# The end of the router in another order, and products of ones behind the last expert

## The chip, the cores and the metric

The kernel runs on one core of a Trainium2 chip, as one program. TensorE (PE) does matrix products and turns tiles (a transpose is a product with the identity), VectorE (DVE) and ScalarE (ACT) work elementwise, GpSimd (POOL) and SyncE (SP) mostly start DMAs. The metric is the device time of one execution in microseconds, the median of several.

## What is computed

A decoder trunk of two layers over 576 tokens (512 of a prompt, 64 of samples), 1024 wide. The part that the change touches is the hierarchical mixture of experts, which follows the mixer in each layer:

```
x = layer_norm(ALPHA * x + mix)                     # x1
g_logits = x @ w_group + b_group                    # 4 groups
e_logits = x @ w_expert + b_expert                  # 16 experts
g_idx = argmax(g_logits)
top_vals, top_idx = top_k(e_logits of group g_idx, 2)
hgu = x @ w_gate_up[e];  a = silu(gate) * up * combine;  y = sum over e of a @ w_down[e]
x = layer_norm(ALPHA * x + y)                       # x2
x = x + sigmoid(x @ w_gate + b) * (p[i] @ w_proj)   # gate products, projection
```

## The kernel before

Every product is made in float32 quality from two halves of each operand (`hi`, the rounded part, and `lo`, the rest), as three products: ACT makes `w_hi` or `x_hi`, DVE subtracts to get `lo`. The program is written by hand for each engine: each engine has its own list of instructions, works through it strictly in the written order, and waits on semaphores (`wait_ge`). So the order of the calls below is the order in time.

The mixer's last products are made token by token (`out_rows`). The 576 tokens are five tiles, 0 to 3 of 128 tokens and 4 of 64. For tile i TensorE does `row_turns(i)` (x added by a turn), then `row_products(i, h, ...)` for the two halves h of the 1024 columns, 12 products each. Then follows the router for that tile:

- DVE: `stats_of(i)` and `norm_of(i)`, the layer norm, which gives `x_tok` (semaphore `normed`, `nz_ok`); ACT supplies the square root in between (`std_tile`).
- PE: `h_turns(i)` turns the 128 x 1024 rows into PSUM banks 4 and 5, which all tiles share, so it waits until the tile before is out of them (`hl_ok`).
- ACT: `rows_hi(i)` copies out `x1T_hi`; DVE: `rows_lo(i)` subtracts to `x1T_lo`.
- PE: `logits(i)`, 16 narrow products. Tiles 0 and 1 are group 0, tiles 2 to 4 group 1 (`GROUPS`).
- for a group g: ACT `logits_copy(g)`, PE `logit_turns(g)`, DVE the choice of experts (`select`: comparisons, places, one-hot marks), PE `ranks(g)` (a running count of the tokens of each expert), DVE `slots_of(g)`, PE `slot_products(g)`. They end in `slot_token` (`idx`), the list of which token stands in which slot of which expert.

With that list POOL gathers the 128 rows of the first expert from `x_scratch` into `x_gathered` (an indirect DMA), PE turns them (`turn_slots`), and the 16 experts begin (`gate_up`). While the router has TensorE wait, the projection of `p` (eight tiles of 12 products, `proj_half`/`proj`, copied out by ACT in `proj_out`) fills in: tiles 1 and 0 before and around the last logits, tile 2 around the slot products, tiles 3 to 6 while the gather is under way, tile 7 behind `turn_slots`.

The weights of the experts come in units of 1 MB. SP starts a load when DVE has split the unit that stood in the slot (`split_done`), so the loads follow the pace of the other engines.

Behind the last expert, `last_rows` adds the last two experts' rows on TensorE, DVE and ACT make the second layer norm tile by tile (`add_rows`, `row_mean`, `squares`, `std_of`, `rstd2`), TensorE turns the tiles (`n2_turn_rows(i)`), DVE and ACT scale them into `xT` and split them, and the sixteen `gate(q)` products of 24 matmuls each follow. `n2_turn_rows(2)` stands behind `gate(1)`, `n2_turn_rows(3)` behind `gate(4)`.

Of the kernel before, what the change touches and what calls it, by code (L numbers as in the profile page):

```python
# [79 lines left out]
def trunk(nc, x_in, outs):  # L80
# [228 lines left out]
    with ctx:  # L309
# [38 lines left out]
        ht_ok, hh_ok, hl_ok = sem("x1_turned"), sem("x1T_hi_ready"), sem("x1T_lo_ready")  # L348
        lt_cp, lt_ok = sem("logits_copied"), sem("logits_turned_back")
# [64 lines left out]
        def rows_bank(i):  # L414
            return 2 * (i % 2)
# [11 lines left out]

        def p_parts(dst, g):
# [70 lines left out]

        TR_IN = 0  # L500
# [346 lines left out]
        def _(act):  # L847
# [74 lines left out]
            for l in range(DEPTH):  # L922
# [10 lines left out]

                def proj_out(mo):
                    act.wait_ge(mt_done, M_P[l] + (1, 0, 2, 3, 4, 5, 6, 7).index(mo) + 1)
                    act.activation(halves(ppT[:, mo, :]), pair(mo % 2), ACT.Copy).then_inc(pp_done, 1)
# [31 lines left out]
                rows_hi(4)  # L968
                logits_copy(1)
                proj_out(1)  # L970
                proj_out(0)
                hi(U_E[l] + 1)
                proj_out(2)
                hi(U_E[l] + 2)
                for mo in range(3, KT - 1):
                    proj_out(mo)
# [186 lines left out]
        def _(dve):  # L1163
# [149 lines left out]
            for l in range(DEPTH):  # L1313
# [23 lines left out]

                def p_low(g):
# [7 lines left out]

                lg20 = lg[:, :, :, :].rearrange("p t g j -> p t (g j)")

                def select(a, b):
# [12 lines left out]
                    for c, (op, mask) in enumerate(((ALU.is_ge, earlier), (ALU.is_gt, later))):  # L1362
# [4 lines left out]
                                              in_=won.rearrange("p q c i -> p q (c i)"), op=ALU.add, axis=AX.X))  # L1367
                    place = rank_c[:, 5 * a:5 * b, :].rearrange("p (t g) j -> p t g j", g=5)
# [358 lines left out]
        def _(pe):  # L1727
# [170 lines left out]
            def out_rows(l, gl_n, pair_sem, pair_n, d):  # L1898
# [48 lines left out]

                def logit_turns(g):
# [384 lines left out]
```

## Time and profile before

| | |
|---|---|
| median of 3 runs | 1281.59 us (1281.4 to 1281.94) |
| the profiled execution: time, span | 1281.04 us, 1279.5 us |
| PE busy | 1227.1 us, 96% of the span |
| DVE busy | 834.9 us, 65% |
| ACT busy | 558.0 us, 44% |
| chain that ended last, by engine | PE 71%, DVE 13%, DMA 10%, ACT 3% |
| mean granted clock of TensorE | 0.983 |

A row of the timeline gives the start in us from the span's start, the length in us, the engine, the line of the kernel and the operation, and in brackets the time the engine was idle before it and what ended that.

### The profile page before, as it was taken

The page shows a single profiled execution, that of the slowest core. Times are in us where ns is not written, and L with a number is a line of the kernel's source. Part 1 is how long each engine was busy: PE and PEld are TensorE (multiplying, and loading weights), DVE is VectorE, ACT ScalarE, POOL GpSimd, SP SyncE. Part 2 cuts the span into 40 slices and gives each one's busy share as a digit, 9 for nine tenths or more (in the row PEclk, how much of TensorE's full clock was granted, in tenths as well). Part 3 has the DMA queues.
Part 4 walks back from the last instruction along what each step waited for, and adds up shares of the span by engine and source line. Part 5 has one row for each costly group of instructions (what it writes and reads, how often), then busy time and mean ns, then how long its engine had stood idle before and what let it go on. Part 6 is the DMA issues. An engine that isn't in the chain of part 4 may idle for free.

```text
span 1279.5 us, 19633 instructions
## 1 busy us (share of the span) xinstructions
PE 1227.1 (96%) x7659; PEld 1115.6 (87%) x7659; DVE 834.9 (65%) x1118; ACT 558.0 (44%) x627; POOL 164.0 (13%) x193
## 2 busy tenths in 40 slices
PE   7999999999999999899999799999999899999798
PEld 6888899999999998788878599999998788877598
DVE  4554477464474737789889785445434778989783
ACT  4322232213131222378787564112121368878651
POOL 2200010010000002013231001000002012232100
PEclk9999999999999999799999899999999899999899
DMA  9444254243242322469998553322312359999512
GB/s 337 153 158 156 104 158 144 93 150 119 78 152 73 126 77 101 161 259 378 374 377 302 195 168 101 99 67 93 105 69 85 141 198 366 388 396 346 211 50 75
DMA packets 85616, 229.76 MB, mean 180 GB/s; under 512 B 9798, under 2 KB 42702, under 8 KB 73136
## 3 DMA queue, kind: packets, MB, share of 16 engines
q1 hardware_dynamic: 66880, 179.84, 38.9%
q0 software_dynamic: 18672, 49.04, 10.8%
q8 instruction: 44, 0.72, 0.2%
q14 instruction: 20, 0.16, 0.0%
HBM read 210.15 MB, written 35.46 MB: 192 GB/s over the span
## 4 chain that ended last, share of the span: by engine, by line
PE 71%; DVE 13%; DMA 10%; ACT 3%; issue 2%; POOL 1%; DVEq 0%; SPq 0%; POOLq 0%; ACTq 0%
PE ps L1739 14%; PE ps L1741 14%; PE ps L1740 14%; DMA w_raw<-in_moe_w_gate_up 7%; PE ps L1790 3%; PE ps L1792 3%; PE ps L1791 3%; DVE w_lo L1169 3%; PE ps L2077 2%; PE ps L2079 2%; PE ps L2078 2%; ACT w_hi L853 2%; PE ps L1850 2%; DVE x_tok L1568 2%; PE ps L2041 1%
## 5 line engine op out<-in xcount | busy, mean ns | idle before, releaser
L1169 DVE TENSOR_TENSOR w_lo<-w_raw,w_hi 128x2048 fp32r<-128x2048 f32 (+1 forms) x133 | 290.5, 2191 | 70.4 <-ACT w_hi L853 69.6
L1739 PE MATMUL ps<-x_hi,w_hi 128*128 128x288 f32 (+2 forms) x1024 | 306.4, 299 | 8.8 <-DVE x_lo L1613 7.1
L1741 PE MATMUL ps<-x_hi,w_lo 128*128 128x288 f32 (+2 forms) x1024 | 303.9, 297 | 0.0
L1740 PE MATMUL ps<-x_lo,w_hi 128*128 128x288 f32 (+2 forms) x1024 | 303.9, 297 | 0.0
L853 ACT ACTIVATE w_hi<-w_raw 128x2048 fp32r<-128x2048 f32 (+1 forms) x133 | 242.7, 1834 | 79.3 <-PE ps L1741 61.6
L1739 PEld LDWEIGHTS ps<-x_hi,w_hi 128*128 128x128 f32 x1024 | 195.0, 190 | 9.9 <-issue 7.5
L1740 PEld LDWEIGHTS ps<-x_lo,w_hi 128*128 128x128 f32 x1024 | 194.9, 190 | 0.1
L1741 PEld LDWEIGHTS ps<-x_hi,w_lo 128*128 128x128 f32 x1024 | 194.8, 190 | 0.0
L1739 PE MATMUL ps<-g_hi,w_hi 128*128 128x288 f32 x384 | 114.8, 299 | 3.4 <-DVE g_full L1715 2.7
L1741 PE MATMUL ps<-g_hi,w_lo 128*128 128x288 f32 x384 | 113.9, 296 | 0.0
L1740 PE MATMUL ps<-g_lo,w_hi 128*128 128x288 f32 x384 | 113.7, 296 | 0.0
L2077 PE MATMUL ps<-w_hi,xgT_hi 128*128 128x512 f32 x256 | 103.1, 403 | 6.7 <-DVE xgT_lo L1460 6.5
L2079 PE MATMUL ps<-w_hi,xgT_lo 128*128 128x512 f32 x256 | 100.2, 391 | 0.0
L2078 PE MATMUL ps<-w_lo,xgT_hi 128*128 128x512 f32 x256 | 99.7, 390 | 0.0
L1790 PE MATMUL ps<-w_hi,x_hi 128*128 128x512 f32 x192 | 75.8, 395 | 3.5 <-DVE w_lo L1180 3.5
L1739 PEld LDWEIGHTS ps<-g_hi,w_hi 128*128 128x128 f32 x384 | 72.7, 189 | 5.0 <-DVE g_full L1715 2.9
L1169 DVE TENSOR_TENSOR w_lo<-w_raw_more,w_hi 128x2048 fp32r<-128x2048 f32 x30 | 68.1, 2291 | 13.0 <-ACT w_hi L853 13.0
L1792 PE MATMUL ps<-w_hi,x_lo 128*128 128x512 f32 x192 | 75.4, 393 | 0.0
L1791 PE MATMUL ps<-w_lo,x_hi 128*128 128x512 f32 x192 | 75.3, 392 | 0.0
L1254 DVE TENSOR_TENSOR gate_sum<-ps,b_spatial 128x512 f32<-128x512 f32 x24 | 16.5, 690 | 89.2 <-PE ps L1852 89.2
L1741 PEld LDWEIGHTS ps<-g_hi,w_lo 128*128 128x128 f32 x384 | 72.7, 189 | 0.0
L1740 PEld LDWEIGHTS ps<-g_lo,w_hi 128*128 128x128 f32 x384 | 72.7, 189 | 0.0
(295 smaller groups left out, 2123.3 us busy)
## 6 DMA issues: line engine op xcount, KB each, us to landing
w_raw<-in_moe_w_gate_up SPq DMA_DIRECT2D x34, 1024.0 KB, 11.0
w_raw<-in_moe_w_down SPq DMA_DIRECT2D x32, 1024.0 KB, 13.8
w_raw_more<-in_moe_w_gate_up SPq DMA_DIRECT2D x30, 1024.0 KB, 14.3
w_raw<-in_a_w_in SPq DMA_DIRECT2D x23, 1024.0 KB, 5.2
w_raw<-in_a_w_out SPq DMA_DIRECT2D x12, 1024.0 KB, 5.1
w_raw<-in_b_w_in SPq DMA_DIRECT2D x12, 1024.0 KB, 5.2
w_raw<-in_ple_w_gate SPq DMA_DIRECT2D x8, 1024.0 KB, 11.9
v_scratch<-v_stage POOLq DMA_DIRECT2D x6, 1024.0 KB, 4.5
```

The lines of the kernel that those rows point to most:

```text
L853: act.activation(unit_of(whi, d), raw_unit(d), ACT.Copy).then_inc(hi_done, 1)
L1169: dve.tensor_tensor(unit_of(wlo, d), raw_unit(d), unit_of(whi, d).bitcast(f32), ALU.subtract).then_inc(split_done, 1)
L1568: ch.link(dve.scalar_tensor_tensor(out=xtok[0:t, i, :], in0=yrows(i, t, k), scalar=wtop[0:t, k, i:i + 1], in1=xtok[0:t, i, :], op0=ALU.mul ...
L1739: pe.matmul(out, sh, mh, start=first, stop=False)
L1740: pe.matmul(out, sh, ml, start=False, stop=False)
L1741: ins = pe.matmul(out, sl, mh, start=False, stop=final)
L1790: pe.matmul(v_bank(i), xh_, wh, start=first, stop=False)
L1791: pe.matmul(v_bank(i), xh_, wl, start=False, stop=False)
L1792: ins = pe.matmul(v_bank(i), xl_, wh, start=False, stop=final)
L2077: pe.matmul(ps[:, 0, :], xs[0], ws[0], start=(a == 0 and k == 0), stop=False)
L2078: pe.matmul(ps[:, 0, :], xs[0], ws[1], start=False, stop=False)
L2079: ins = pe.matmul(ps[:, 0, :], xs[1], ws[0], start=False, stop=(a == 1 and k == 3))
```

## The change

At the router's end the order is rewritten on three engines, in both layers. On PE `h_turns(3)` goes between the two halves of the row products of tile 4, `logit_turns(0)` just ahead of it. On DVE `rows_lo(3)` goes ahead of the norm of tile 4. `select` is cut in two, `places_of` and `marks_of`, and the marks of group 0 come behind the norm of tile 4. The tile 4 is normed, turned, copied, subtracted and multiplied in two halves of 512 columns, with a semaphore for each first half (`norm_last`, `last_turns`, `last_rows_hi`, `last_rows_lo`, `last_logits`). The projection's tiles run in the order 1, 0, 3, 2, 4 to 7; tile 3 comes ahead of the ranks, so that tiles 4 to 6, not 3 to 6, stand between the slot products and `turn_slots`. Behind the last expert 6, 6 and 12 products of ones with ones, 512 columns wide, are written into PSUM bank 0; nothing reads them, and the first of `gate(0)` overwrites the bank.

```
+        PROJ_ORDER = (1, 0, 3, 2, 4, 5, 6, 7)
...
+                def last_rows_hi():
+                    act.wait_ge(r_mm, NT * l + NT - 2)
+                    for h, (turned_ok, done) in enumerate(((ht_half, hh_half), (ht_ok, hh_ok))):
+                        act.wait_ge(turned_ok, (l + 1) if h == 0 else NT * (l + 1))
+                        act.activation(hTh[0][:, 4 * h:4 * h + 4, 0:TS], turned_half(h), ACT.Copy).then_inc(done, 1)
...
+                def norm_last():
...
+                    for h, done in enumerate((nz_half, nz_ok)):
+                        c = slice(512 * h, 512 * h + 512)
+                        dve.scalar_tensor_tensor(out=xtok[0:TS, i, c], in0=xtok[0:TS, i, c], scalar=rstd[0:TS, i:i + 1], in1=lnp[0:TS, 1, c],
+                                                 op0=ALU.mult, op1=ALU.add).then_inc(done, 1)
...
-                select(*GROUPS[0])
+                places_of(*GROUPS[0])
+                rows_lo(3)
                 stats_of(4)
-                norm_of(4)
-                rows_lo(3)
-                rows_lo(4)
+                norm_last()
+                marks_of(*GROUPS[0])
+                last_rows_lo()
                 slots_of(*GROUPS[0])
-                select(*GROUPS[1])
+                places_of(*GROUPS[1])
+                marks_of(*GROUPS[1])
                 slots_of(*GROUPS[1])
                 lo(U_E[l] + 1)
...
                 h_turns(2)
+                row_products(4, 0, range(ROUND))
                 logit_turns(0)
-                row_products(4, 0, range(ROUND))
+                h_turns(3)
                 row_products(4, 1, range(ROUND)).then_inc(mt_done, KT - NT + 1)
-                h_turns(3)
                 pe.wait_ge(pl_ok, 3 * l + 3)
                 logits(2)
-                ranks(0)
-                pe.wait_ge(nz_ok, 2 * NT * l + NT - 1)
                 proj_half(l, 1, 0)
                 proj_half(l, 1, 1).then_inc(mt_done, 1)
-                h_turns(4)
                 logits(3)
-                logits(4)
-                pe.wait_ge(nz_ok, 2 * NT * l + NT)
+                last_turns()
+                ranks(0)
                 proj_half(l, 0, 0)
+                last_logits()
+                proj_half(l, 0, 1).then_inc(mt_done, 1)
                 logit_turns(1)
-                proj_half(l, 0, 1).then_inc(mt_done, 1)
+                pe.wait_ge(pp_done, KT * l + 1)
+                proj_half(l, 3, 0)
+                proj_half(l, 3, 1).then_inc(mt_done, 1)
+                pe.wait_ge(pp_done, KT * l + 2)
+                proj_half(l, 2, 0)
                 ranks(1)
                 slot_products(0)
-                pe.wait_ge(pp_done, KT * l + 2)
-                proj_half(l, 2, 0)
+                proj_half(l, 2, 1).then_inc(mt_done, 1)
                 slot_products(1).then_inc(ab_used, 1)
-                proj_half(l, 2, 1).then_inc(mt_done, 1)
-                for mo in range(3, KT - 1):
+                for mo in range(4, KT - 1):
                     proj(l, mo)
                 turn_slots(l, 0, bank=4)
                 proj(l, KT - 1)
...
+                def keep_running(n):
+                    for _ in range(n):
+                        pe.matmul(ps[:, 0, :].rearrange("p (a t) -> p a t", t=P), ones_r[:, :],
+                                  ones_r[:, :].unsqueeze(1).to_broadcast([P, 4, P]), start=True, stop=True)
+
+                pe.wait_ge(atl_ok, NE * (l + 1))
+                keep_running(6)
                 n2_turn_rows(0)
+                keep_running(6)
                 n2_turn_rows(1)
-                pe.wait_ge(atl_ok, NE * (l + 1))
+                keep_running(12)
                 for q in range(GQ):
                     gate(q)
```

On DVE, at the router's end, the order was as follows, from the marks of group 0 to the ranks of its slots (`x1T_lo_121` and `x1T_lo_120` are the lower halves of the turned rows of tile 3 and of tile 4):

```order
L1372 SCALAR_TENSOR_TENSOR expert_onehot<-places,group_onehot 128x32
L1375 SCALAR_TENSOR_TENSOR choice_onehot<-places,group_onehot 128x32 x2
L1379 TENSOR_TENSOR choice_rows<-choice_onehot,row_value 128x32 x2
L1322 BN_STATS v_stats<-ps 64x6 x2
L1324 BN_AGGR mean_var<-v_stats 64x2
L1330 SCALAR_TENSOR_TENSOR x_tok<-ps,mean_var,ln_params 64x1024
L1333 RECIPROCAL rstd<-rstd 64x1
L1335 SCALAR_TENSOR_TENSOR x_tok<-x_tok,rstd,ln_params 64x1024
L1345 TENSOR_TENSOR x1T_lo_121<-ps,x1T_hi_119 128x1024
L1345 TENSOR_TENSOR x1T_lo_120<-ps,x1T_hi_118 128x8x64
L1389 TENSOR_TENSOR choice_values<-choice_onehot,ps 128x32 x2
```

and it is now:

```order
L1371 TENSOR_TENSOR x1T_lo_121<-ps,x1T_hi_119 128x1024
L1335 BN_STATS v_stats<-ps 64x6 x2
L1337 BN_AGGR mean_var<-v_stats 64x2
L1354 SCALAR_TENSOR_TENSOR x_tok<-ps,mean_var,ln_params 64x1024
L1357 RECIPROCAL rstd<-rstd 64x1
L1361 SCALAR_TENSOR_TENSOR x_tok<-x_tok,rstd,ln_params 64x512 x2
L1404 SCALAR_TENSOR_TENSOR group_onehot<-places,valid 128x8
L1407 SCALAR_TENSOR_TENSOR expert_onehot<-places,group_onehot 128x32
L1410 SCALAR_TENSOR_TENSOR choice_onehot<-places,group_onehot 128x32 x2
L1414 TENSOR_TENSOR choice_rows<-choice_onehot,row_value 128x32 x2
L1376 TENSOR_TENSOR x1T_lo_120<-ps,x1T_hi_118 128x4x64 x2
L1424 TENSOR_TENSOR choice_values<-choice_onehot,ps 128x32 x2
```

The tile 3 is subtracted ahead of the statistics of tile 4 and no longer behind its norm, the marks of group 0 stand behind the norm in place of ahead of it, and the last scaling and the last subtraction are two instructions each.

On PE, between the row products of tile 4 (`w_hi,g_hi`), the turns (`x_tok`) and the logits, the list was:

```order
L1935 MATMUL ps<-ident,x_tok 128x128 x8
L1953 MATMUL ps<-ident,logits_turned 128x64 x2
L1915 MATMUL ps<-w_hi,g_hi 64x512
L1916 MATMUL ps<-w_lo,g_hi 64x512
...
L1916 MATMUL ps<-w_lo,g_hi 64x512
L1917 MATMUL ps<-w_hi,g_lo 64x512
L1935 MATMUL ps<-ident,x_tok 128x128 x8
L1944 MATMUL ps<-x1T_hi_118,w_router_hi_lo 64x128
```

and it is now:

```order
L1972 MATMUL ps<-ident,x_tok 128x128 x8
L1952 MATMUL ps<-w_hi,g_hi 64x512
L1953 MATMUL ps<-w_lo,g_hi 64x512
...
L1954 MATMUL ps<-w_hi,g_lo 64x512
L2007 MATMUL ps<-ident,logits_turned 128x64 x2
L1972 MATMUL ps<-ident,x_tok 128x128 x8
L1952 MATMUL ps<-w_hi,g_hi 64x512
L1953 MATMUL ps<-w_lo,g_hi 64x512
```

The turn of tile 3 stands ahead of the second twelve products in place of behind them, and the turn of the logits of group 0 behind the first twelve in place of ahead of them.

On PE, behind the last expert (`last_onehot` are the marks of `last_rows`, `x_tok` the rows that `n2_turn_rows` turns, `x_hi` and `w_hi` the first gate products), the list was:

```order
L2135 MATMUL ps<-expert_y,last_onehot 128x512 x8
L2197 MATMUL ps<-ident,x_tok 128x128 x16
L1739 MATMUL ps<-x_hi,w_hi 128x256
L1740 MATMUL ps<-x_lo,w_hi 128x256
L1741 MATMUL ps<-x_hi,w_lo 128x256
```

and it is now, with the products of ones:

```order
L2189 MATMUL ps<-expert_y,last_onehot 128x512 x8
L2286 MATMUL ps<-ones_r 128x512 x6
L2251 MATMUL ps<-ident,x_tok 128x128 x8
L2286 MATMUL ps<-ones_r 128x512 x6
L2251 MATMUL ps<-ident,x_tok 128x128 x8
L2286 MATMUL ps<-ones_r 128x512 x12
L1776 MATMUL ps<-x_hi,w_hi 128x256
L1777 MATMUL ps<-x_lo,w_hi 128x256
L1778 MATMUL ps<-x_hi,w_lo 128x256
```

One run of 16 transposes is now cut into two of 8, with unread products ahead of each and behind.

## Rows read from the trace of the kernel before

**Rows 1.** The page, part 4: the chain's share of the span by line.
```profile
...
PE ps L1739 14%; PE ps L1741 14%; PE ps L1740 14%; DMA w_raw<-in_moe_w_gate_up 7%; PE ps L1790 3%; PE ps L1792 3%; PE ps L1791 3%; DVE w_lo L1169 3%; PE ps L2077 2%; PE ps L2079 2%; PE ps L2078 2%; ACT w_hi L853 2%; PE ps L1850 2%; DVE x_tok L1568 2%; PE ps L2041 1%
...
```

**Rows 2.** Windows: stretch, its length, each engine's busy time, PEclk, DMA share, GB/s.
```profile
...
528.00:540.00 12.00, 10.83 (x48) 10.09 (x48) 7.37 (x22) 3.42 (x4) 0.00 (x0) 0.50 0.08 33
540.00:550.00 10.00, 9.79 (x72) 9.36 (x71) 6.70 (x24) 6.06 (x10) 3.11 (x3) 1.00 0.74 264
...
```

**Rows 3.** Timeline of TensorE, router's end, layer 0: start, length, what, [idle before <-releaser].
```profile
...
513.08 0.45 PE L1915 MATMUL ps<-w_hi,g_hi 128*64 128x512 f32 x1
...
518.67 1.04 PE L1935 MATMUL ps<-ident,x_tok 128*128 128x128 f32 x8
519.47 0.30 PE L1944 MATMUL ps<-x1T_hi,w_router_hi_lo 128*64 128x128 f32 x1
...
524.38 0.68 PE L1935 MATMUL ps<-ident,x_tok 64*128 64x64 f32 x8 [1.84 <-DVE x1T_lo L1345]
...
526.47 0.31 PE L1944 MATMUL ps<-x1T_hi,w_router_hi_lo 128*64 128x64 f32 x1 [0.31 <-DVE x1T_lo L1345]
...
533.41 0.45 PE L1968 MATMUL ps<-expert_onehot,below_r 128*128 128x96 f32 x1 [1.17 <-DVE expert_onehot L1372]
...
538.32 0.55 PE L1739 MATMUL ps<-pT_hi,w_hi 128*128 128x288 f32 x1
...
539.87 0.31 PE L1739 MATMUL ps<-pT_hi,w_hi 128*128 128x288 f32 x1
...
546.42 0.75 PE L2041 MATMUL ps<-ident,x_gathered 128*128 128x128 f32 x5
```

**Rows 4.** Timeline of VectorE, the same stretch.
```profile
...
518.88 1.29 DVE L1322 BATCH_NORM_STATS2 v_stats<-ps 64x6 f32<-64x512 f32 x2
...
521.82 1.28 DVE L1335 SCALAR_TENSOR_TENSOR x_tok<-x_tok,rstd,ln_params 64x1024 f32<-64x1024 f32 x1
523.03 1.21 DVE L1345 TENSOR_TENSOR x1T_lo<-ps,x1T_hi 128x1024 fp32r<-128x1024 f32 x1
...
530.54 0.22 DVE L1353 SCALAR_TENSOR_TENSOR logits<-ps,b_router 128x60 f32<-128x60 f32 x1 [2.82 <-PE ps L1953]
...
536.60 2.29 DVE L1169 TENSOR_TENSOR w_lo<-w_raw,w_hi 128x2048 fp32r<-128x2048 f32 x1
...
539.01 0.17 DVE L1430 SCALAR_TENSOR_TENSOR slot_token<-choice_shift,ps 128x16 uint32<-128x16 f32 x1
...
```

**Rows 5.** Timeline of GpSimd: the first gather of layer 0.
```profile
...
540.12 1.12 POOL L791 DMA_INDIRECT x_gathered<-x_scratch,slot_token  x1 [16.18 <-DVE slot_token L1430]
...
```

**Rows 6.** Tile x_gathered, window of the first gather, then the whole run.
```profile
...
DMA to landing us min/median/max: 5.4/5.4/5.4
...
DMA to landing us min/median/max: 4.1/8.7/10.9
...
```

**Rows 7.** Timeline of TensorE in the short convolution: products behind a long wait.
```profile
...
915.84 0.61 PE L1739 MATMUL ps<-g_hi,w_hi 128*128 128x288 f32 x1 [2.67 <-DVE g_full L1715]
...
918.84 0.29 PE L1739 MATMUL ps<-g_hi,w_hi 128*128 128x288 f32 x1
...
```

**Rows 8.** Timeline of TensorE behind the last expert, layer 0.
```profile
...
716.79 1.09 PE L2197 MATMUL ps<-ident,x_tok 128*128 128x128 f32 x8 [1.69 <-ACT x_tok L1061]
719.50 1.09 PE L2197 MATMUL ps<-ident,x_tok 128*128 128x128 f32 x8 [1.61 <-DVE x_tok L1586]
724.13 0.55 PE L1739 MATMUL ps<-x_hi,w_hi 128*128 128x256 f32 x1 [3.54 <-DVE x_lo L1613]
...
727.79 0.28 PE L1741 MATMUL ps<-x_hi,w_lo 128*128 128x256 f32 x1
...
731.38 0.28 PE L1741 MATMUL ps<-x_hi,w_lo 128*128 128x256 f32 x1
732.83 1.06 PE L2197 MATMUL ps<-ident,x_tok 128*128 128x128 f32 x8 [1.17 <-DVE x_tok L1586]
...
747.13 0.38 PE L1739 MATMUL ps<-x_hi,w_hi 128*128 128x256 f32 x1 [0.87 <-DVE w_lo L1169]
...
```

More of the change, by code:

```diff
@@ L1336, in norm_of @@
                                              op0=ALU.mult, op1=ALU.add).then_inc(nz_ok, 1)
+                def norm_last():
+                    i, b = NT - 1, rows_bank(NT - 1)
+                    dve.wait_ge(st_ok, NT * (l + 1))
+                    dve.scalar_tensor_tensor(out=xtok[0:TS, i, :], in0=ps[0:TS, b:b + 2, :].rearrange("p b t -> p (b t)"), scalar=mv[0:TS, i, 0:1],
+                                             in1=lnp[0:TS, 0, :], op0=ALU.subtract, op1=ALU.mult).then_inc(rs_ok, 1)
+                    dve.wait_ge(sq_ok, 1 + n1 + NT)
+                    ch.link(dve.reciprocal(rstd[0:TS, i:i + 1], rstd[0:TS, i:i + 1]))
+                    dve.wait_ge(rs_ok, 1 + n1 + NT)
+                    for h, done in enumerate((nz_half, nz_ok)):
+                        c = slice(512 * h, 512 * h + 512)
+                        dve.scalar_tensor_tensor(out=xtok[0:TS, i, c], in0=xtok[0:TS, i, c], scalar=rstd[0:TS, i:i + 1], in1=lnp[0:TS, 1, c],
+                                                 op0=ALU.mult, op1=ALU.add).then_inc(done, 1)
                 def p_low(g):
@@ L1345, in rows_lo, with last_rows_lo, places_of @@
                     dve.tensor_tensor(hTl[i % 2][:, :, 0:tok(i)], turned(i), hTh[i % 2][:, :, 0:tok(i)].bitcast(f32), ALU.subtract).then_inc(hl_ok, 1)
+                def last_rows_lo():
+                    for h, (hi_ok, done) in enumerate(((hh_half, hl_half), (hh_ok, hl_ok))):
+                        dve.wait_ge(hi_ok, (l + 1) if h == 0 else NT * (l + 1))
+                        dve.tensor_tensor(hTl[0][:, 4 * h:4 * h + 4, 0:TS], turned_half(h), hTh[0][:, 4 * h:4 * h + 4, 0:TS].bitcast(f32),
+                                          ALU.subtract).then_inc(done, 1)
                 lg20 = lg[:, :, :, :].rearrange("p t g j -> p t (g j)")
-                def select(a, b):
+                def places_of(a, b):
                     n, g = b - a, (0 if a == 0 else 1)
@@ L1946, in logits, with last_turns, last_logits @@
                     ins.then_inc(r_mm, 1)
+                def last_turns():
+                    pe.wait_ge(hl_ok, NT * l + NT - 1)
+                    for h, (normed, done) in enumerate(((nz_half, ht_half), (nz_ok, ht_ok))):
+                        pe.wait_ge(normed, (l + 1) if h == 0 else 2 * NT * l + NT)
+                        for k in range(4 * h, 4 * h + 4):
+                            ins = pe.transpose(ps[:, 4 + h, (k % 4) * P:(k % 4) * P + TS], xtok[0:TS, NT - 1, k * P:k * P + P], ident[0:TS, 0:TS])
+                        ins.then_inc(done, 1)
+                def last_logits():
+                    out = ps[0:RW, 7, P * (NT - 1 - GROUPS[1][0]):P * (NT - 1 - GROUPS[1][0]) + TS]
+                    for h, lo_ok in enumerate((hl_half, hl_ok)):
+                        pe.wait_ge(lo_ok, (l + 1) if h == 0 else NT * (l + 1))
+                        for k in range(4 * h, 4 * h + 4):
+                            pe.matmul(out, wrp[:, k, :], hTh[0][:, k, 0:TS], start=(k == 0), stop=False)
+                            ins = pe.matmul(out, wrp[:, k, :], hTl[0][:, k, 0:TS], start=False, stop=(k == KT - 1))
+                    ins.then_inc(r_mm, 1)
                 def logit_turns(g):
```

18 lines of the change are left out of this document (12 added, 6 removed).

## The prediction

> **What bounds the kernel now.** I read the chain of waits first: most of it is TensorE's products, and the loads of the experts' weights hold 7% [rows 1]. SP starts each of those loads when DVE has split the unit before, so they follow whatever comes ahead of them: a shift at the router's end passes through the experts to the end of the layer.
>
> Then the windows by stage. At the end of the router TensorE runs at the lower of its two levels, granted 0.50 (1.2 GHz), from 528 to 540, and at 1.00 from 540 to 550 [rows 2]. So every product there is dear: six projection products take 1.55 us (538.32 to 539.87, 0.26 each), while the 48 products of tiles 3 to 6 behind them take 6.55 us (539.87 to 546.42), 0.136 each [rows 3]. The factor is 1.9.
>
> Then the timelines of TensorE and VectorE in that stretch. The reader is to see a chain that goes to and fro. TensorE has the row products of tile 4 from 513.08 to 518.67, then the turn of tile 3 [rows 3]. DVE takes statistics of tile 4 from 518.88, scales it at 521.82, and subtracts tile 3 from 523.03 to 524.24 [rows 4]; only then is the turn of tile 4 let go, 524.38, behind 1.84 us of idle time that x1T_lo of tile 3 ends [rows 3]. The last logits start at 526.47, the choice of experts at 530.54, the ranks at 533.41, DVE writes slot_token at 539.01 [rows 3, 4], and POOL issues the gather at 540.12 [rows 5], which lands 5.4 us later [rows 6], at 545.5. `turn_slots` follows at 546.42 without idle time, since the projection fills it [rows 3]. Layer 1 runs the same program; I take it to be the same stretch, and count each gain twice.
>
> Last the layer's end. There TensorE waits 1.69, 1.61 and 3.54 us for the layer norm on DVE and ACT, then falls behind no more than 1.17 and 0.87 us later on [rows 8].
>
> **The router's end, step by step (times of layer 0).**
> 1. The turn of tile 3 now stands inside the row products of tile 4; it occupies TensorE from 518.67 to 519.47 [rows 3]. The products end 0.8 us later, and so does the statistics of tile 4: 519.7. The logits' turn moves too, within the same products, at nothing. The norm of tile 4 ends 0.8 later, 523.9, its first half at 523.3 [rows 4].
> 2. The subtraction of tile 3 (1.21 us [rows 4]) is done by 519.3, beneath those products: turned by 516.9 (twelve products of 5.59/24 = 0.233 us behind 513.08, then 1.04 [rows 3]), then ACT's copy, about 1. So the 16 logit products of tile 3 leave the path too.
> 3. Tile 4 goes in halves. Its second half is turned, copied and subtracted behind 523.9 in about 1.8 us; before, it was 524.38 to 526.47 for the whole, 2.1 us [rows 3]. Second half of the last logits: 525.7 against 526.47. The marks of group 0 lie in DVE's wait for ACT.
> 4. From the last logits to the choice of experts are now 4.07 us (526.47 to 530.54 [rows 3, 4]) of narrow products, half a projection tile and turns at the lower clock. By the factor 1.9 they are 2.1 at the higher, and 8 of the 16 narrow products are ahead already (0.4): 1.7 to 1.8. Choice at 527.5, 3.0 us earlier. That asks for the clock to stay up; TensorE's idle time ahead of the turn of tile 4 is filled by tile 3's logits and the second projection half.
> 5. The choice takes what it took, 2.87 us (530.54 to 533.41): ranks at 530.4. Tile 3 of the projection and half of tile 2 fill that (18 x 0.136 = 2.4).
> 6. From the ranks to the free DVE behind the slot marks were 3.19 us (533.41 to 536.60 [rows 3, 4]). The six rank products at full clock save about 0.7: 532.9. The slot products on TensorE end at about 533.9, before 538.5.
> 7. On DVE the split of a weight unit, w_lo, still stands ahead of slot_token, 2.41 us from 536.60 to 539.01 [rows 4]. It now ends last: slot_token at 535.3, 3.7 us earlier. The gather is issued at 536.4 and lands, by 5.4 us, at 541.8.
> 8. `turn_slots` starts at 541.8 to 542.7 (before, 0.9 us lay between the landing and it, all of it busy [rows 3]); I take 542.2, a gain of 4.2.
> 9. New wait: only tiles 4 to 6 stand ahead of it, 36 x 0.136 = 4.9 us behind 533.9, so TensorE is out of work at 538.8 and idles 3.4 us. What the wait costs is its effect on the clock. The nearest row is the convolution's: behind 2.67 us of idle time, twelve products take 3.00 us (915.84 to 918.84 [rows 7]) against 12 x 0.136 = 1.63. Cost 1.4 us, bounds 0 and 6.3 (below). The Trainium skill says the same in TensorE: Matmul & The Clock Gate, "HAM oscillation — how this bites in real kernels": a wait for a DMA between bursts of products makes the next burst begin at the low clock. By that rule the sum stays as it is, and the trace agrees [rows 7].
> 10. The gather shares the way with weight loads that are let go earlier as well. Bounds: 0, and the run's median landing of 8.7 in place of 5.4, so 3.3 [rows 6]. I take 0.5, near the first gather's own row, since it ran beside a 1 MB load already. The Trainium skill, DMA: Bandwidth & Descriptors, "Issuing engines are not separate DMA queues", holds that queues of all engines end in the same 16 DMA engines and interleave there. By it the value leans to the upper bound; no row shows a gather alone.
>
> Sum per layer: -4.2 + 1.4 + 0.5 = -2.3 us.
>
> The rest at this place I cost at nothing. Two instructions for one on DVE add some 0.1 us each, within the waits on ACT; without these they would cost 0.2. The semaphores of the projection's banks are met by then. POOL's write of the rows waits 0.8 us longer, beneath 16 us in which POOL waits anyway [rows 5]. The loads of the next weights start 3 us earlier and lengthen nothing but the gather.
>
> **The products of ones.** One such product is priced by the row products, also 512 wide: 0.233 us [rows 3]. Six are 1.4 us, in waits of 1.69 and 1.61; twelve are 2.8, in 3.54 [rows 8]. So they fit where nothing waits for TensorE. They may keep the clock up: `gate(0)` begins with 17 products in 3.66 us (724.13 to 727.79), 0.215 each, then 30 in 3.59 (727.79 to 731.38), 0.12 each [rows 8]. At full clock TensorE would be 17 x 0.095 = 1.6 us earlier. But then it waits for DVE's x_tok of tile 2, at 732.83, where 1.17 us of idle time show that DVE ends last [rows 8]. The gain is swallowed and the wait grows to 2.8 us. Worth: zero, as long as DVE doesn't move. Bounds: a gain of 0, and a loss of 1.2 per layer, if the grown wait (2.67 was enough in the convolution) lets the clock fall: 1.4, less a little of the 0.87 wait behind it.
>
> **Total.** 1281.04 us is the profiled execution's own time (span 1279.5 and 1.5 around it). Twice -2.3 gives 1276.4. The median of the runs lies 0.55 above the profiled one, so 1277.0.
>
> **Rivals.**
> - The clock falls behind the first gates. For it: the wait of 2.8 us [rows 7]. Against: it follows two gates at full clock and 8 transposes stand in between. +1.2 per layer, 1279.4.
> - The whole gain comes: no clock lost at the gather's wait, no contention. -4.2 per layer less a little, 1273.2. For it: the wait follows 4.9 us of dense products. Against: rows 7's products too came after busy stretches.
> - The gather collides: it takes the median 8.7 us. -4.2 + 3.3 + 1.4 = +0.5 per layer, 1282.6, no change. Against: only one or two loads are due then.
> - The other side, slower: the wait for the gather brings the long low stretch from the router's end into the first expert. In the kernel before the low clock lasts from about 526.47 to 539.87, 13.4 us [rows 3], in which products with gaps don't raise it. 13.4 x (1 - 0.136/0.26) = 6.3 us of work lost; -4.2 + 0.5 + 6.3 = +2.6 per layer, 1286.8. It decides from where the low clock outlasts 7.9 us of products (3.7/0.47). Against: `turn_slots`, projection tile 7 and the first expert are dense.
> - The change doesn't do what it says: the clock falls before the last logits as before. Then the order alone is left, about 0.8 from step 3 and 0.4 from the 8 logit products taken off: -1.2 per layer, and the projection still covers the gather. 1279.2.
>
> **How the numbers follow.** Chances: forecast 0.50, its own range 1274.8 to 1279.0 (contention 0 to 1, start of `turn_slots` 541.8 to 542.7, in two layers); clock behind the gates 0.18; whole gain 0.13; collision 0.07; the order alone 0.07; slower 0.05. The range from 1273.2 to 1280.2 leaves out the collision, the slow case and little of the tails. 0.2%, about what a measurement of this kernel can tell from no change, is 2.6 us: faster ends at 1279.0, slower starts at 1284.2. Faster holds the forecast, the whole gain and part of the two cases at 1279.2 and 1279.4: 0.70. Slower: 0.05. The rest, 0.25, is no change.
>
> **What would show it.** In the profile after: a granted clock of 1.00 through the router's end, no idle time of 1.8 us ahead of the turn of tile 4, the choice near 527.5, slot_token near 535.3, then TensorE idle for some 3.4 us with x_gathered as the one that ends it, `turn_slots` near 542.2 with longer products behind it, the landing of the first gather below 6.5 us. Behind the last expert: products of 0.12 from `gate(0)` on, and an idle time of 2.8 us ahead of the turn of tile 2. I am wrong if the granted clock falls at the router's end all the same, if the products of ones run at half clock (12 x 0.44 = 5.3 us, more than the wait of 3.54), or if the split of the weights, and not the rows, holds the first expert, which would swallow the gain.

## The result, and the profile after

The changed kernel takes 1284.26 us (median of 20 runs, 1281.14 to 1286.28), the kernel before 1281.63 in its 20. The ratio is 1.0017, interval 1.0011 to 1.0024: slower by 0.17%, some 2.2 us (the two medians lie 2.6 us apart), where 0.36% faster was forecast. That is above 1280.2, the range's upper end. Its profiled execution took 1282.73 us (span 1281.2), 1.7 more than the profiled one of before, and TensorE's mean granted clock rose from 0.983 to 0.993: the mean clock rose, and the time was lost all the same.

Windows of the changed kernel (stretch, length, busy times of PE, PEld, DVE, ACT, POOL, then PEclk, DMA share, GB/s):

```profile
...
526.20:539.90 13.70, 12.84 (x103) 11.91 (x102) 11.73 (x35) 7.19 (x8) 2.33 (x1) 1.00 0.49 175
...
545.00:548.40 3.40, 3.30 (x15) 3.30 (x16) 1.34 (x3) 1.30 (x3) 0.55 (x1) 0.51 0.11 43
...
732.70:736.10 3.40, 3.40 (x18) 3.40 (x17) 3.33 (x5) 1.05 (x1) 0.00 (x0) 0.50 0.00 0
1034.90:1039.90 5.00, 4.98 (x21) 4.98 (x22) 2.83 (x11) 1.59 (x5) 0.99 (x1) 0.50 0.08 12
...
```

The router's end, at 0.50 in [rows 2], now runs at 1.00. But the low clock is back at three places behind it, each full of products: 545.0, 732.7 and 1034.9.

The timeline of TensorE of the changed kernel, the same stretch as [rows 3]:

```profile
...
524.22 1.03 PE L1990 MATMUL ps<-ident,x_tok 64*128 64x64 f32 x8 [0.32 <-DVE x_tok L1361]
...
531.48 0.31 PE L2022 MATMUL ps<-expert_onehot,below_r 128*128 128x96 f32 x1 [0.33 <-DVE expert_onehot L1407]
...
534.17 0.89 PE L2014 MATMUL ps<-choice_rows,slot_onehot 128*128 128x128 f32 x6 [0.51 <-DVE slot_onehot L1430]
...
539.32 0.30 PE L1776 MATMUL ps<-pT_hi,w_hi 128*128 128x288 f32 x1
...
545.10 1.98 PE L2096 MATMUL ps<-ident,x_gathered 128*128 128x128 f32 x8 [5.22 <-DMA x_gathered<-x_scratch,slot_token]
...
549.15 0.39 PE L2131 MATMUL ps<-w_hi,xgT_hi 128*128 128x512 f32 x1
...
```

The wait ahead of the turn of tile 4 fell from 1.84 to 0.32 us, the ranks start at 531.48 in place of 533.41, and the slot products at 534.17. Then comes what was not forecast: 5.22 us of idle time ahead of `turn_slots`, which starts at 545.10, and its eight turns take 1.98 us in place of 1.1. The first expert starts at 549.15; in the kernel before it did so at 549.34:

```profile
...
549.34 0.47 PE L2077 MATMUL ps<-w_hi,xgT_hi 128*128 128x512 f32 x1 [0.21 <-DVE xgT_lo L1460]
...
```

Why the gather is late shows when DVE, GpSimd and SP are laid beside each other. DVE, GpSimd and SP of the changed kernel, then the time to landing of the first gather of either layer:

```profile
...
536.44 0.17 DVE L1467 SCALAR_TENSOR_TENSOR slot_token<-choice_shift,ps 128x16 uint32<-128x16 f32 x1
...
536.62 2.28 DVE L1182 TENSOR_TENSOR w_lo<-w_raw,w_hi 128x2048 fp32r<-128x2048 f32 x1
...
```

```profile
...
537.55 2.33 POOL L797 DMA_INDIRECT x_gathered<-x_scratch,slot_token  x1 [11.98 <-DVE slot_token L1467]
...
```

```profile
...
536.49 0.34 SPq L588 DMA_DIRECT2D w_raw<-in_moe_w_gate_up  x1
539.07 0.33 SPq L588 DMA_DIRECT2D w_raw<-in_moe_w_down  x1
```

```profile
...
DMA to landing us min/median/max: 7.5/7.5/7.5
...
DMA to landing us min/median/max: 8.1/8.1/8.1
...
```

slot_token is there at 536.44, 2.6 us earlier than in [rows 4], and DVE goes on at once with the next split of a weight unit, 536.62 to 538.90. GpSimd's row of the gather, 1.12 us in [rows 5], is now 2.33 us long and ends 0.98 us behind that split. At 539.07 SP starts a second load of 1 MB, which the split let go; the first started at 536.49. The gather lands 7.5 us behind its start in layer 0 and 8.1 in layer 1, against 5.4 in [rows 6].

In the kernel before the second split couldn't come there. ACT's copy of that unit stood behind the copy of projection tile 2, which came late. ACT (the copy of tile 2, then that of the unit), DVE and SP of the kernel before:

```profile
...
540.08 0.65 ACT L936 ACTIVATE ple_projT<-ps 128x576 f32<-128x576 f32 x1 [5.36 <-PE ps L1741]
540.63 1.91 ACT L853 ACTIVATE w_hi<-w_raw 128x2048 fp32r<-128x2048 f32 x1
...
```

```profile
...
542.57 2.29 DVE L1169 TENSOR_TENSOR w_lo<-w_raw,w_hi 128x2048 fp32r<-128x2048 f32 x1 [3.31 <-ACT w_hi L853]
...
```

```profile
...
545.04 0.33 SPq L582 DMA_DIRECT2D w_raw<-in_moe_w_down  x1
```

DVE stood idle for 3.31 us while GpSimd made the gather's descriptors, and the second load started at 545.04, when the gather was about to land. The change moved both copies forward, and this cover was gone. ACT of the changed kernel:

```profile
...
533.70 0.65 ACT L948 ACTIVATE ple_projT<-ps 128x576 f32<-128x576 f32 x1 [2.42 <-PE ps L1778]
534.25 1.91 ACT L859 ACTIVATE w_hi<-w_raw 128x2048 fp32r<-128x2048 f32 x1
...
```

The layer's end in the changed kernel, as [rows 8] (`ones_r` are the unread products):

```profile
...
716.41 1.09 PE L2251 MATMUL ps<-ident,x_tok 128*128 128x128 f32 x8 [0.39 <-ACT x_tok L1074]
...
719.12 1.09 PE L2251 MATMUL ps<-ident,x_tok 128*128 128x128 f32 x8 [0.21 <-DVE x_tok L1623]
719.97 2.99 PE L2286 MATMUL ps<-ones_r 128*128 128x512 f32 x12
723.75 0.36 PE L1776 MATMUL ps<-x_hi,w_hi 128*128 128x256 f32 x1 [0.79 <-DVE x_lo L1650]
...
732.45 1.75 PE L2251 MATMUL ps<-ident,x_tok 128*128 128x128 f32 x8 [2.72 <-DVE x_tok L1623]
...
748.24 0.39 PE L1776 MATMUL ps<-x_hi,w_hi 128*128 128x256 f32 x1 [0.79 <-DVE w_lo L1182]
...
```

The products of ones fill the waits as forecast, `gate(0)` starts at 723.75 with products at full clock, and TensorE then waits 2.72 us for x_tok of tile 2. Behind this wait the eight turns take 1.75 us in place of 1.06, and the first gate product behind DVE's w_lo stands at 748.24, 15.8 us behind the turns, where it was 14.3.

Where the 1.7 us of the two profiled executions arise, from the starts of the same instruction in both timelines:

| place | before | after | difference |
|---|---|---|---|
| first turns of the router, layer 0 | 493.91 | 494.54 | +0.63 |
| `turn_slots`, layer 0 | 546.42 | 545.10 | -1.32 |
| turn of the second expert, layer 0 | 554.86 | 554.61 | -0.25 |
| turn of tile 2, layer's end 0 | 732.83 | 732.45 | -0.38 |
| turn of tile 3, layer's end 0 | 742.36 | 743.54 | +1.18 |
| first turns of the router, layer 1 | 982.35 | 983.80 | +1.45 |
| `turn_slots`, layer 1 | 1034.85 | 1034.92 | +0.07 |
| turn of the second expert, layer 1 | 1043.26 | 1045.19 | +1.93 |
| last turns, layer's end 1 | 1237.84 | 1239.52 | +1.68 |

The first 0.63 lies ahead of everything that was changed. The router gains 1.95 and 1.4 us up to `turn_slots`, the first expert gives back 1.1 and 1.9, and the layer's end loses 1.6 in layer 0 and gains 0.25 in layer 1. That the median lies 1.5 us above this profiled execution is taken up with the experiments.

### The profile page after: what moved, and what is told of

Read it like the earlier page. It is cut to its first block, busy times and chain, and to the rows that moved or that the text cites. A ratio compares the mean times of both kernels' runs of the same rounds, so it can differ in the third digit from the quotient of the medians.

```text
span 1281.2 us, 19733 instructions
## 1 busy us (share of the span) xinstructions
PE 1229.9 (96%) x7707; PEld 1116.9 (87%) x7707; DVE 835.6 (65%) x1122; ACT 559.4 (44%) x629; POOL 166.8 (13%) x193
## 4 chain that ended last, share of the span: by engine, by line
PE 69%; DMA 13%; DVE 11%; ACT 3%; issue 2%; POOL 1%; DVEq 0%; SPq 0%; POOLq 0%; ACTq 0%
PE ps L1776 14%; PE ps L1778 14%; PE ps L1777 14%; DMA w_raw<-in_moe_w_gate_up 9%; PE ps L1827 3%; PE ps L1828 3%; PE ps L1829 3%; DVE w_lo L1182 3%; ACT w_hi L859 2%; PE ps L2131 2%; PE ps L2133 2%; PE ps L2132 2%; PE ps L1887 2%; DMA x_gathered<-x_scratch,slot_token 1%; DVE x_tok L1605 1%
## 6 DMA issues: line engine op xcount, KB each, us to landing
w_raw<-in_moe_w_gate_up SPq DMA_DIRECT2D x34, 1024.0 KB, 10.8
```

## The experiments

**The theory:** three things ate the gain. The second split holds up GpSimd and lets a second load run beside the gather; the longer wait puts the low clock where it counts, behind the gather; and the products of ones let the clock fall behind the layer's first gates. **The rivals:** the gather's length comes from the first load alone, or the descriptors alone, or the products of ones are harmless and all is lost at the router. All ratios below are to the kernel before on the same chip; the kernel before had a median of 1281.39 us in the first group of four, 1282.24 in the second and 1282.77 in the third. Kernels of one group ran on one chip and are compared by their ratios. A ratio is not the quotient of the two medians and differs from it by up to 0.0009, so that effects of 1 or 2 us come out unlike by the two: e2 costs 1.9 us by its ratio and 1.1 by the medians. The fastest kernels were run least: e9 has 4 executions, e5, e7 and e8 have 5 each, e6 has 6 and e3 7, against 11 or 12 of the others. One of the 29 executions of the kernel before in group 1 took 6814 us, which nothing explains; the median is untouched by it.

| run | group | median us | ratio | interval |
|---|---|---|---|---|
| e1_no_ones | 1 | 1281.89 | 1.0004 | 0.9995 to 1.0013 |
| e2_ones_alone | 1 | 1282.46 | 1.0015 | 1.0006 to 1.0024 |
| e3_split_behind | 1 | 1276.78 | 0.9970 | 0.9959 to 0.9982 |
| e4_load_held | 1 | 1278.61 | 0.9984 | 0.9974 to 0.9995 |
| e5_split_behind_no_ones | 2 | 1276.21 | 0.9947 | 0.9933 to 0.9962 |
| e6_ones_in_wait | 2 | 1276.83 | 0.9952 | 0.9935 to 0.9970 |
| e7_both | 2 | 1274.96 | 0.9945 | 0.9932 to 0.9958 |
| e8_list_first | 2 | 1273.27 | 0.9921 | 0.9908 to 0.9935 |
| e9_list_first_no_ones | 3 | 1271.01 | 0.9904 | 0.9890 to 0.9919 |
| e10_changed_again | 3 | 1284.60 | 1.0016 | 1.0005 to 1.0026 |
| e11_tile3_behind | 3 | 1281.40 | 0.9989 | 0.9980 to 0.9998 |
| e12_no_ones_again | 3 | 1283.13 | 0.9998 | 0.9989 to 1.0007 |

### The split behind the gather: e3 and e4

e3 moves one instruction of DVE:

```
                 dve.tensor_scalar(row_idx[:, 0:NE], row_v, -1.0, 2.0 * T, ALU.mult, ALU.add).then_inc(row_ok, 1)
-                lo(U_E[l] + 2)
...
                 dve.scalar_tensor_tensor(out=row_late[:, :], in0=last_at[:, 2, :], scalar=2.0 * T, in1=late_v, op0=ALU.add, op1=ALU.subtract)
+                lo(U_E[l] + 2)
```

> The changed kernel with one instruction of DVE moved: the second split of a weight unit behind slot_token (2.28 us, at 536.62 in the changed kernel) goes behind the slots' last small operations, about 4 us of them, and with it the load that it lets go. Theory A (that split holds up GpSimd while it makes the gather's descriptors, 2.33 us in place of 1.12, and lets a second load of 1 MB run beside the gather): GpSimd's row of the first gather back to about 1.1 us, its landing 5.4 to 6 us behind its start in place of 7.5 and 8.1, turn_slots 1.5 to 2.5 us earlier in each layer, and 2 to 5 us less than the changed kernel in all. Theory B (the gather's length has to do with the weight load that comes first, at 536.5, alone): GpSimd's row stays at 2.3, landing 7 or more, time within 0.7 us of the changed kernel's.

e4 holds only the load:

```
                         sp.wait_ge(split_done, last_user + 1 if it is None else it * 12 + (last_user + 1))
+                        if e == 7:
+                            sp.wait_ge(xg_ld[0], 16 * ((NE // 2) * l + 1))
```

> The changed kernel, in which SyncE holds the load of the experts' unit 7 (the one that started at 539.07, beside the gather) until the first gather has landed; DVE's order is untouched. Theory A (two costs: the descriptors on GpSimd, and the loads): GpSimd's row of the gather stays at 2.3 us, and the landing behind it goes from 5.2 back towards 4.3 us, so turn_slots 0.9 us earlier and 0 to 2 us less in all. Theory B (it is the load alone): GpSimd's row shortens too. Theory C (the load has no part): the landing stays at 7.5 and 8.1 us.

The first gather on GpSimd, `turn_slots` on TensorE and the second load on SP, of e3:

```profile
...
536.65 1.12 POOL L797 DMA_INDIRECT x_gathered<-x_scratch,slot_token  x1 [11.97 <-DVE slot_token L1467]
...
```

```profile
...
541.73 1.23 PE L2096 MATMUL ps<-ident,x_gathered 128*128 128x128 f32 x8 [2.73 <-DMA x_gathered<-x_scratch,slot_token]
...
```

```profile
...
540.57 0.33 SPq L588 DMA_DIRECT2D w_raw<-in_moe_w_down  x1
```

and of e4:

```profile
...
536.94 2.33 POOL L799 DMA_INDIRECT x_gathered<-x_scratch,slot_token  x1 [11.97 <-DVE slot_token L1469]
...
```

```profile
...
542.45 1.23 PE L2098 MATMUL ps<-ident,x_gathered 128*128 128x128 f32 x8 [3.17 <-DMA x_gathered<-x_scratch,slot_token]
...
```

```profile
...
542.63 0.33 SPq L590 DMA_DIRECT2D w_raw<-in_moe_w_down  x1
```

With the split out of the way GpSimd's row is 1.12 us again, with the load held alone it stays at 2.33: the split and nothing else lengthens it. `turn_slots` starts behind the gather's start by 5.1 us in e3, 5.5 in e4, and 7.55 in the changed kernel. So of the 2.5 us the second load holds 2.05, and the split beyond it 0.4; in layer 1 it is 2.4 and 0.5 (5.3 us in e3, 5.7 in e4, 8.1 in the changed kernel). I had expected 0.9 of the load. Against the changed kernel's ratios of 1.0017 and 1.0016 (neither measured beside e3 and e4) e3 takes about 6 us less and e4 about 4, more than the 2 to 5 and 0 to 2 expected. The load's 2.05 and 2.4 are the whole of e4's. The 2.5 and 2.9 of both together are five of e3's six. The rest fits the clock: the wait fell from 5.22 to 2.73 us, and from `turn_slots` to the turn of the second expert e3's profiled execution takes 8.5 and 9.7 us in the two layers, the changed kernel's 9.5 and 10.3.

What the Trainium skill says on this, in SBUF — State Buffer, "Who interferes with whom": a DVE instruction with two inputs in SBUF contends with a GpSimd instruction that reads SBUF. The split has two such inputs and the gather reads its list there; the trace agrees, 2.33 against 1.12 us, and the row's end follows the split's.

### The products of ones: e1, e2, e12

e1 and e12 are the changed kernel without them, e2 is the kernel before with them alone, e10 the changed kernel again. The edit, in e1 and e12:

```
...
-                pe.wait_ge(atl_ok, NE * (l + 1))
-                keep_running(6)
                 n2_turn_rows(0)
-                keep_running(6)
                 n2_turn_rows(1)
-                keep_running(12)
+                pe.wait_ge(atl_ok, NE * (l + 1))
```

and in e2 its reverse on the kernel before.

> The changed kernel without its 24 unread products of ones per layer; nothing else is touched. Theory A (the ones are a loss: they bring the first gates forward, TensorE then waits 2.72 us for DVE in place of 1.17, and the clock falls behind that wait, which made layer 0's end 1.5 us longer): 1.5 to 3 us less than the changed kernel's 1284.3, so 1281.3 to 1282.8, and in the profile a stretch of 0.50 at the first gates and none behind the turn of tile 2. Theory B (the ones are harmless and the whole loss is at the router's end): 1284.3 within 0.7.

> The kernel before with the 24 products of ones per layer alone, the router as it was. Theory A (the ones are a loss of 1.2 to 1.5 us in each layer in which the clock falls behind the grown wait): 1282.8 to 1284.6. Theory B (harmless): 1281.6 within 0.7. Theory C (they gain what the first 17 gate products lose at the lower clock, 1.6 us a layer): 1278.5.

> The changed kernel without the products of ones behind the last expert, again, beside the changed kernel on one chip. Theory A (the ones are a loss of 1 to 2 us in all): 1 to 2.5 us less than the changed kernel's run of the same chip. Theory B (harmless): within 0.7 of it.

> The changed kernel itself, beside the same without the ones, on one chip. Both theories: ratio to the kernel before 1.001 to 1.003.

Without the ones the changed kernel is level with the kernel before, 1.0004 and 0.9998, and on one chip 0.0018 below itself (e12 against e10: 2.3 us, 1.5 by the medians). The ones alone cost 0.0015, interval 0.0006 to 0.0024, 1.9 us; e2's median, 1282.46, lies just below the 1282.8 to 1284.6 of theory A. The profiled execution of e2 had no fall of the clock there and showed no cost.

The traces of all kernels together show why. The wait ahead of the turn of tile 2 is 2.71 or 2.72 us at all 16 layer ends with the ones (eight kernels, two layers each), and 0.34 to 1.25 at all 12 without. From that turn to the turn of tile 3 it is 9.53 or 9.54 us at the 12 without and at 7 of the 16 with them. At the other 9 it is 10.89 to 11.11, and the granted clock is 0.52 to 0.71 just behind the turn of tile 2. So the same wait of 2.7 us brings the clock down at some layer ends and not at others, and each time it costs 1.4 to 1.6 us. Nine in sixteen at 1.5 us are, by my estimate, 1.7 us in an execution with two layers, near the 1.9 and 2.3 measured. One of each, from e3's two layers, the turns of tile 2 and of tile 3 (11.07 us apart, then 9.54):

```profile
...
727.29 1.05 PE L2251 MATMUL ps<-ident,x_tok 128*128 128x128 f32 x6 [2.71 <-DVE x_tok L1623]
...
738.36 1.03 PE L2251 MATMUL ps<-ident,x_tok 128*128 128x128 f32 x8
...
1213.83 1.06 PE L2251 MATMUL ps<-ident,x_tok 128*128 128x128 f32 x8 [2.71 <-DVE x_tok L1623]
...
1223.37 1.03 PE L2251 MATMUL ps<-ident,x_tok 128*128 128x128 f32 x8
...
```

TensorE at the layer's end in e12:

```profile
...
724.74 0.55 PE L1776 MATMUL ps<-x_hi,w_hi 128*128 128x256 f32 x1 [3.54 <-DVE x_lo L1650]
...
733.45 0.74 PE L2251 MATMUL ps<-ident,x_tok 128*128 128x128 f32 x5 [0.34 <-DVE x_tok L1623]
```

`gate(0)` begins with products of 0.55 us, at the lower clock, behind the wait of 3.54, and TensorE still waits for DVE (0.34) at the turn of tile 2. There the low clock costs nothing. Theory A holds: e1 lies within the 1281.3 to 1282.8 expected, and e12 within its 1 to 2.5 us below e10.

### Ones in the wait for the gather: e5, e6, e7

e5 is e3 without the ones behind the last expert. e6 is e3 with ten products of ones in the wait, e7 is e5 with them:

```
+                pe.wait_ge(pp_done, KT * l + KT - 2)
+                for _ in range(10):
+                    pe.matmul(ps[:, 2, :].rearrange("p (a t) -> p a t", t=P), ones_r[:, :],
+                              ones_r[:, :].unsqueeze(1).to_broadcast([P, 4, P]), start=True, stop=True)
                 turn_slots(l, 0, bank=4)
```

> The kernel with the second split moved (1276.8), and without the products of ones behind the last expert. Theory A (with them the clock falls behind the grown wait of 2.7 us in a part of the executions, and a fall there isn't hidden; without them it falls behind the wait of 3.5 us, where DVE ends last anyway): 1274 to 1276.2. Theory B (harmless): 1276.8 within 0.7.

> The kernel with the second split moved (1276.8), and ten unread products of ones per layer between projection tile 6 and turn_slots, written into a PSUM bank that the last projection tile overwrites. They take 2.2 us of a wait of 2.7 to 2.9. Theory A (the wait for the gather brings the clock down behind it, which costs up to 1.4 us in each layer): no stretch of 0.50 at the first expert, 1274 to 1276. Theory B (in this kernel the wait is already short enough in most executions): within 0.7 of 1276.8. If the ten products delay turn_slots: slower by up to 1.

> The second split moved, ten products of ones in the wait for the gather, and none behind the last expert. If both theories A hold: 1272.5 to 1275, the fastest so far. If neither: 1276.8 within 0.7.

TensorE in e7:

```profile
...
539.84 2.45 PE L2089 MATMUL ps<-ones_r 128*128 128x512 f32 x10
542.70 1.23 PE L2100 MATMUL ps<-ident,x_gathered 128*128 128x128 f32 x8 [0.40 <-DMA x_gathered<-x_scratch,slot_token]
...
```

The ten products fit, and the wait is down to 0.40 us. But e7 and e5 are level, 0.9945 and 0.9947, and e7's median only just reaches the upper end of what was expected. e6 lies at the 1276.8 of its theory B, and e5, at 1276.21, lies where its two theories meet. Neither e6 nor e7 has a low stretch behind the gather in its profiled execution, but e5 has none either: its waits there are 1.02 us in layer 0, where the clock had fallen at the slot products already (0.65 from 534 to 537), and 2.65 in layer 1. In e3's there was one, in layer 1, behind a wait of 2.90. So there was little left to save. The intervals reach 0.0013 to 0.0018 to either side, so a gain of a microsecond can't be told here; below that the experiment is inconclusive. The pair e5 against e3, 0.9947 and 0.9970, has the sign of a loss by the ones behind the last expert, but the two ran on different chips; e7 against e6, on one chip, has it too, within the noise.

### The list of slots first: e8, e9

e8 is e3 with the first split moved too; e9 is the same without the ones behind the last expert:

```
-                lo(U_E[l] + 1)
                 dve.wait_ge(ab_used, l + 1)
...
                 dve.scalar_tensor_tensor(out=row_late[:, :], in0=last_at[:, 2, :], scalar=2.0 * T, in1=late_v, op0=ALU.add, op1=ALU.subtract)
+                lo(U_E[l] + 1)
                 lo(U_E[l] + 2)
```

> The kernel with the second split moved (1276.8), and the first split moved as well, from ahead of slot_token to ahead of the second, behind the slots' small operations; the products of ones stay behind the last expert. slot_token can then come 1.5 to 2.2 us earlier, until the slot products on TensorE end last. Theory A (that split stands on the path to the gather): the gather starts 1.5 us earlier, TensorE's wait ahead of turn_slots falls from 2.8 to about 1.3 us, and the time by 1.5 to 3 us, to 1273.8 to 1275.3. Theory B (the first expert waits for its weights, whose split now ends later, or the next loads are late): the gain at turn_slots is given back by the first experts, 1276 to 1278.

> The kernel with both splits behind the list of slots (ratio 0.9921 to the kernel before), without the products of ones behind the last expert. Theory A (the ones cost 1 to 2 us in all, as in the pairs so far): ratio 0.9906 to 0.9914, near 1270. Theory B (harmless once the router is mended): 0.9921 within 0.0005.

GpSimd and TensorE of e8:

```profile
...
536.74 1.12 POOL L797 DMA_INDIRECT x_gathered<-x_scratch,slot_token  x1 [10.84 <-DVE slot_token L1466]
...
```

```profile
...
541.09 1.23 PE L2096 MATMUL ps<-ident,x_gathered 128*128 128x128 f32 x8 [0.88 <-DMA x_gathered<-x_scratch,slot_token]
...
544.44 0.47 PE L2131 MATMUL ps<-w_hi,xgT_hi 128*128 128x512 f32 x1 [0.54 <-DVE xgT_lo L1497]
...
```

The wait for the gather is 0.88 us. Two things shorten it. The list comes 3.8 us behind the ranks in place of e3's 4.95, 1.1 us earlier and not the 1.5 to 2.2 expected. And the first load, which the moved split lets go, now starts at 540.64 by SP's timeline, 3.9 us behind the gather's start: `turn_slots` follows that start by 4.35 us, in place of 5.1 in e3. In layer 1 it is 4.6 and 5.3. So even the one load beside the gather had its price: in the kernel before it landed after 5.4 and 5.2 us, in e9, without that load, after 4.3 and 4.2. The first expert now waits 0.54 us for its own rows on DVE, behind the two splits, but not for weights. e8 is 0.0026 below e5 on the same chip although it still has the ones, and somewhat better than expected. e9 reaches 0.9904, just below the 0.9906 to 0.9914 expected: 12 us less than the kernel before, and 12 less than e12, which differs from it by the place of the two splits alone, on the same chip. Most of it shows in the profiled executions. From the ranks to the turn of the second expert e9 takes 18.2 and 18.1 us in the two layers, e12 24.1 and 23.2, together 11.0 us more. It is the fastest version found.

### The spread projection: e11

The changed kernel with tile 3 back behind the slot products (ACT's copies and the counts waited for follow, not shown):

```
-        PROJ_ORDER = (1, 0, 3, 2, 4, 5, 6, 7)
+        PROJ_ORDER = (1, 0, 2, 3, 4, 5, 6, 7)
...
-                pe.wait_ge(pp_done, KT * l + 1)
-                proj_half(l, 3, 0)
-                proj_half(l, 3, 1).then_inc(mt_done, 1)
...
-                for mo in range(4, KT - 1):
+                for mo in range(3, KT - 1):
```

> The changed kernel with the projection's tile 3 back behind the slot products: TensorE waits 1.6 us longer ahead of the ranks, and 1.6 less for the gather, 3.6 in place of 5.2. The gather itself is as in the changed kernel, and still lands 7.5 us behind its start. Theory A (the wait for the gather is set by the landing; what matters is only how long the clock is low behind it): turn_slots at the same time, a shorter or no stretch of 0.50 behind it, 0 to 2 us less than the changed kernel. Theory B (the wait's length makes no odds): within 0.7 of it. Theory C (the wait ahead of the ranks brings the clock down there): 1 to 3 us more.

TensorE of e11, then its windows:

```profile
...
530.68 0.31 PE L2021 MATMUL ps<-expert_onehot,below_r 128*128 128x96 f32 x1 [1.44 <-DVE expert_onehot L1406]
...
544.33 1.23 PE L2092 MATMUL ps<-ident,x_gathered 128*128 128x128 f32 x8 [0.89 <-DMA x_gathered<-x_scratch,slot_token]
...
```

```profile
...
532.70:539.40 6.70, 6.27 (x28) 6.03 (x27) 6.53 (x13) 3.10 (x3) 2.35 (x2) 0.50 0.39 132
544.40:548.00 3.60, 3.46 (x23) 3.16 (x24) 2.18 (x8) 1.26 (x4) 0.99 (x1) 1.00 0.09 31
...
```

The wait ahead of the ranks is 1.44 us and the clock falls behind it, as theory C said, in both layers. Yet e11 is 0.0027 (3.5 us) faster than the changed kernel on the same chip, more than the 0 to 2 of theory A. The low clock from 532.7 to 539.4 costs nothing: slot_token hangs on DVE and comes 4.96 us behind the ranks in e11 as in e10, and the gather's landing covers the slower projection. That projection, at the lower clock, is also why the wait ahead of `turn_slots` is 0.89 us and not the 3.6 expected. The turns take 1.23 us, and from there to the turns of the second expert are 8.5 us (544.33 to 552.84), against 10.4 in e10 (544.88 to 555.25) and 8.4 in the kernel before. In layer 1 they are 8.5 against 10.8. So theory A, with the clock's fall of theory C beside it at no price: what counts is on which side of the gather the low stretch lies.

## Why the prediction was wrong

- **Steps 1 to 7, to slot_token: right in kind, a little too high.** 3.7 us were forecast; slot_token came at 536.44 against 539.01, 2.6, or 3.2 when the 0.63 is taken off by which the profiled execution was late before. In layer 1 it was 3.4. The granted clock stayed at 1.00 as step 4 asked.
- **Step 10, the gather beside the loads, failed.** It took 0.5 us "since it ran beside a 1 MB load already". The order of ACT had changed behind it: tile 2 of the projection is copied out early, so the next unit is copied, split and its place refilled just while the gather is on its way. Nothing in the steps followed that chain; the text only says that loads start 3 us earlier "and lengthen nothing but the gather". The landing took 2.1 us more than before in layer 0 (7.5 for 5.4) and 2.9 in layer 1 (8.1 for 5.2). Against the same kernel with the split moved it is 2.5 us in layer 0 (e3), 2.05 of them the load (e4). The rival "the gather collides", given 0.07, named the place and not the mechanism on GpSimd.
- **Step 9: the wait was mis-sized by that, and the clock's price behind it a little too low.** 3.4 us of wait were forecast, 5.22 and 5.74 measured. The price of the clock behind it was put at 1.4; it was 1.1 and 1.9 in the profiled execution, and 1.1 to 2.4, 1.8 on average, over the eight gathers of the changed kernel, e1, e10 and e12, each against the same layer of the kernel before. This and the clock at the layer's end may be why the profiled execution lies below the median. The better choice was there: tile 3 in the wait (e11), since the clock that it keeps up ahead of the ranks is worth nothing.
- **Step 8:** `turn_slots` was to gain 4.2 us, 3.7 with step 10's half; it gained 1.95 and 1.4.
- **The products of ones were valued at zero; measured, they cost about 2 us in all** (e2 1.9, e12 against e10 2.3). The mechanism was the first rival's: the wait of 2.7 us behind full-clock gates, then a low stretch where DVE no longer covers it. The rows for it were there [rows 7, 8]; its chance of 0.18 was too small. Its +1.2 in every layer is 2.4 us, near the total partly by luck: the traces have 1.5 us at nine layer ends of sixteen.
- **The sum.** Forecast -2.3 per layer and 0 for the ones. In the profiled executions the router and the first expert together came to -0.9 in layer 0 and +0.5 in layer 1. Over the runs the router's part without the ones came to nothing (1.0004 and 0.9998 in e1 and e12), and the ones to +2.
- **The slower rival** was not what happened: the low clock behind the gather covered 3.4 us of products in layer 0 and 5.0 in layer 1 (1034.9 to 1039.9), less than the 7.9 us from which it would have decided. The kernel came out slower than before by the gather's landing, the shorter low stretches and the ones together.

## What to carry to other kernels

A mean clock that rises is no gain in itself: ask for each low stretch what covers it, because one under a wait for another engine or a transfer is free, and the same stretch just behind that wait is not. When a copy or product moves forward, follow its semaphore through every queue to the transfer it releases, and look for what is then in flight; here 2 us of a gather went to a weight load that nobody needed yet. Put the short list that starts a transfer ahead of long bulk work on the engine that makes it, and keep long two-input DVE work off the moment in which GpSimd makes descriptors; here that was worth 12 us (e9 against e12), and no product was touched.

## What the runs showed of the hardware

GpSimd's row of the first gather takes 1.11 to 1.12 us in the kernels without a split beside it, and 2.33 to 2.37 when a 128 x 2048 subtraction of DVE with both inputs in SBUF has begun before it; it then ends about 1 us behind that instruction. A gather of 128 rows of 4 KB lands 4.9 to 5.4 us behind its start beside one 1 MB load that began about 1 us before it, where the next load follows 3.9 us behind its start or later and GpSimd's row is not lengthened. It lands after 7.5 to 8.1 when the row is lengthened and a second load follows 1.5 us behind its start. With no load until 3.9 us behind its start it lands after 4.2 to 4.6 (e8, e9). Where the trace has no landing, this is the start of `turn_slots`, which waited for it. All of this held in both layers, the two longer times in the repeated run too. A wait of TensorE of 2.71 or 2.72 us behind the same products was followed by the lower clock at 9 of 16 layer ends.
